# Squares of layer 1's heads summed by two fp32r steps in place of one fp32 matmul

## The reference, cut to what matters

```
proj = h @ w_in[layer]                       # 2048 -> 8 x 1024
q_sb, k_sb, v_sb, z_sb, q_r, k_r, v_r, z_r = jnp.split(proj, split_at, axis=-1)
qa = rms_norm(split_heads(q_sb, 8), sb_q_gain)      # mean of squares over the 128 of a head
ka = rms_norm(split_heads(k_sb, 8), sb_k_gain)
oa = merge_heads(stick_breaking_attention(qa, ka, v)) * silu(z_sb)
...
ob = head_group_norm(chunkwise_retention(qr, kr, vr), ret_norm_gain)   # variance over the 128 of a head
ob = ob * silu(z_r)
x = x + gate * (concatenate([oa, ob]) @ w_out)
```

## Time and profile before

| | us |
|---|---|
| runs | 1768.15, 1771.90, 1775.87 |
| profiled execution, its own time | 1773.34 |
| its span | 1771.5 |
| PE busy | 1726.1 (97%) |
| DVE busy | 1293.4 (73%) |
| ACT busy | 906.5 (51%) |
| POOL busy | 152.3 (9%) |

### The profile page before, as it was taken

The page is one execution under the profiler, slowest core; times in us unless marked ns, Lnnn a source line. Parts: engine busy times, 40 slices in busy tenths (PEclk is TensorE's granted clock), DMA queues, the critical chain, the costliest instruction groups (busy, mean ns, idle before and its releaser), DMA issues.

```text
span 1771.5 us, 24147 instructions
## 1 busy us (share of the span) xinstructions
PE 1726.1 (97%) x9557; PEld 1482.4 (84%) x9557; DVE 1293.4 (73%) x1618; ACT 906.5 (51%) x1176; POOL 152.3 (9%) x177
## 2 busy tenths in 40 slices
PE   7989999999999999999999999999999999999997
PEld 6778888777888888888888888788888888888886
DVE  6889979786788756887677778965554767778653
ACT  6344443444466445665345566644444445566543
POOL 3321101010010100101010010000000000000000
PEclk9989999999999999999999999999999999999999
DMA  9979979774555566667676556556566665544553
GB/s 359 384 273 344 343 228 325 235 242 140 165 167 176 183 178 190 183 186 215 178 215 191 165 167 172 170 185 188 180 186 167 171 197 144 142 131 132 168 188 107
DMA packets 312287, 357.00 MB, mean 202 GB/s; under 512 B 11632, under 2 KB 285168, under 8 KB 312176
## 3 DMA queue, kind: packets, MB, share of 16 engines
q1 hardware_dynamic: 295792, 296.24, 55.3%
q0 software_dynamic: 16384, 59.22, 9.8%
HBM read 353.29 MB, written 2.13 MB: 201 GB/s over the span
## 4 chain that ended last, share of the span: by engine, by line
PE 73%; DVE 14%; ACT 6%; issue 3%; DMA 2%; POOL 1%; SPq 0%; DVEq 0%; ACTq 0%
PE psG L491 41%; PE psG L492 21%; DVE w_lo L421 5%; ACT w_hi L417 3%; PE psG L485 2%; PE psG L487 2%; PE psG L486 2%; DMA raw<-in_mem_w 2%; DVE ada_sum L1289 1%; PE psH L1899 1%; DVE P L1247 1%; PE psH L1913 1%; DVE P L1242 1%; PE psH L1888 0%; PE psH L2079 0%
## 5 line engine op out<-in xcount | busy, mean ns | idle before, releaser
L491 PE MATMUL psG<-xA,w_hi 128*128 128x512 f32 x2624 | 944.4, 403 | 2.5 <-DVE w_lo L421 1.9
L421 DVE TENSOR_TENSOR w_lo<-raw,w_hi 128x1024 fp32r<-128x1024 f32 (+1 forms) x560 | 686.2, 1238 | 228.5 <-ACT w_hi L417 227.0
L492 PE MATMUL psG<-xA,w_lo 128*128 128x256 f32 x2624 | 736.4, 281 | 0.0
L417 ACT ACTIVATE w_hi<-raw 128x1024 fp32r<-128x1024 f32 (+1 forms) x560 | 569.4, 1042 | 238.5 <-PE psG L492 176.4
L491 PEld LDWEIGHTS psG<-xA,w_hi 128*128 128x128 f32 x2624 | 494.4, 188 | 122.2 <-issue 6.3
L492 PEld LDWEIGHTS psG<-xA,w_lo 128*128 128x128 f32 x2624 | 496.9, 189 | 2.3 <-issue 1.4
L491 PE MATMUL psG<-yP,w_hi 128*128 128x512 f32 x960 | 340.6, 399 | 3.4 <-DVE P L1247 1.6
L492 PE MATMUL psG<-yP,w_lo 128*128 128x256 f32 x960 | 269.4, 281 | 0.0
L491 PEld LDWEIGHTS psG<-yP,w_hi 128*128 128x128 f32 x960 | 180.2, 188 | 48.0 <-DVE P L1247 1.9
L460 ACT ACTIVATE P<-psG 128x512 f32<-128x512 f32 (+2 forms) x103 | 60.8, 591 | 239.4 <-PE psG L492 239.4
L492 PEld LDWEIGHTS psG<-yP,w_lo 128*128 128x128 f32 x960 | 181.4, 189 | 0.2
(11 more groups left out here) (331 smaller groups left out, 1777.0 us busy)
## 6 DMA issues: line engine op xcount, KB each, us to landing
raw<-in_w_in SPq DMA_DIRECT2D x360, 512.0 KB, 3.8
raw<-in_w_out SPq DMA_DIRECT2D x128, 512.0 KB, 3.5
ada_ring<-in_w_ada POOLq DMA_DIRECT2D x96, 512.0 KB, 6.2
raw<-in_mem_w SPq DMA_DIRECT2D x32, 512.0 KB, 10.3
raw<-in_w_uq SPq DMA_DIRECT2D x24, 384.0 KB, 3.5
raw<-in_w_ukv SPq DMA_DIRECT2D x32, 128.0 KB, 2.5
raw<-in_w_ukv SPq DMA_DIRECT2D x16, 256.0 KB, 3.4
P<-in_memT SPq DMA_DIRECT2D x4, 512.0 KB, 7.2
```

What stands on the lines that cost most here:

```text
L417: nc.scalar.activation(high(n), low(n, raw), ACT.Copy).then_inc(hi_ready, 1)
L421: nc.vector.tensor_tensor(low(n), low(n, raw), high(n), ALU.subtract).then_inc(lo_ready, 1)
L491: nc.tensor.matmul(psG[:, bank + f, :], hi[:, w], x, start=first, stop=False)
L492: last = nc.tensor.matmul(psG[:, bank + f, S:2 * S], lo[:, w], x[:, 0:S], start=False, stop=end)
```

## The change

The squares are split into a high part in fp32r (ACT, by a copy) and the exact remainder (DVE, by a subtraction), and PE sums both parts with a matrix of ones in fp32r, accumulating into the same bank. `WR` is an fp32r name for the memory of `W`: the high part lies in the second half, the remainder replaces the squares in the first. PE's step moves from p = 2 to p = 3 (retention: p = 12 to 13), ACT's Ln and Exp from p = 3 to 4 (13 to 14). The four semaphores of the dt step are merged into one that counts to 4.

```diff
+        WR = sb("WR", [NP, 2048], F32R, place=top[0])
         W = sb("W", [NP, 2048])
+        ones_r = sb("ones_r", [NP, NP], F32R)
...
@@ ACT
             landed(act, G_SBQK)
+            f(ones_r[:, :], ones, ACT.Copy).then_inc(q["sb_sqh"], 1)
...
                     f(sb_a[:, 512:1024], tiles(n * 2 + SBK, 2), ACT.Square).then_inc(q["sb_sq"], 1)
-                if p == 3:
+                    act.wait_ge(q["sb_sq"], 2 * n + 2)
+                    f(WR[:, 1024:2048], sb_a, ACT.Copy).then_inc(q["sb_sqh"], 1)
+                if p == 4:
                     act.wait_ge(q["sb_ssq"], n + 1)
...
                     f(rt_a[:, 512:1024], rt_a[:, 0:512], ACT.Square).then_inc(q["rt_sq"], 1)
-                if p == 13:
+                    act.wait_ge(q["rt_sq"], n + 1)
+                    f(WR[:, 1024:1536], rt_a[:, 512:1024], ACT.Copy).then_inc(q["rt_sqh"], 1)
+                if p == 14:
                     act.wait_ge(q["rt_var"], n + 1)
@@ DVE
+                if p == 1:
+                    dve.wait_ge(q["sb_sqh"], n + 2)
+                    v.tensor_tensor(WR[:, 0:1024], sb_a, WR[:, 1024:2048], ALU.subtract).then_inc(q["sb_sql"], 1)
...
+                if p == 13:
+                    dve.wait_ge(q["rt_sqh"], n + 1)
+                    v.tensor_tensor(WR[:, 512:1024], rt_a[:, 512:1024], WR[:, 1024:1536], ALU.subtract).then_inc(q["rt_sql"], 1)
@@ PE
-                if p == 2:
-                    pe.wait_ge(q["sb_sq"], n * 2 + 2)
+                if p == 3:
+                    pe.wait_ge(q["sb_sql"], n + 1)
                     if n:
                         pe.wait_ge(q["sb_y"], n)
-                    mm(psH[:, BB, :], ones, sb_a[:, 0:512], start=True, stop=True)
-                    mm(psH[:, BC, :], ones, sb_a[:, 512:1024], start=True, stop=True).then_inc(q["sb_ssq"], 1)
+                    for k in range(2):
+                        mm(psH[:, BB + k, :], ones_r[:, :], WR[:, 1024 + 512 * k:1536 + 512 * k], start=True, stop=False)
+                        ins = mm(psH[:, BB + k, :], ones_r[:, :], WR[:, 512 * k:512 * k + 512], start=False, stop=True)
+                    ins.then_inc(q["sb_ssq"], 1)
...
-                if p == 12:
-                    pe.wait_ge(q["rt_sq"], n + 1)
-                    mm(psH[:, BD, :], ones, rt_a[:, 512:1024], start=True, stop=True).then_inc(q["rt_var"], 1)
+                if p == 13:
+                    pe.wait_ge(q["rt_sql"], n + 1)
+                    mm(psH[:, BD, :], ones_r[:, :], WR[:, 1024:1536], start=True, stop=False)
+                    mm(psH[:, BD, :], ones_r[:, :], WR[:, 512:1024], start=False, stop=True).then_inc(q["rt_var"], 1)
```

More of the change, by code:

```diff
@@ L235, in build @@
             "gate_log gate_lsig gate_sig silc_e ada_cols gate_cols nm_sq nm_pair nm_pre nm_ss nm_ln nm_rs nm_h nm_hi nm_lo "
-            "sb_sq sb_ssq sb_ln sb_rs sb_qk sb_z sb_zs sb_az sb_e sb_l sb_sp sb_S sb_arg sb_w sb_o sb_y "
-            "rt_t0 rt_s rt_qk rt_D rt_z rt_at rt_o rt_os rt_vc rt_sq rt_var rt_ln rt_rs rt_y "
-            "f1_yz f1_y f1_hi f1_lo dt_abs dt_ln dt_cum dt_T mem_col "
+            "sb_sq sb_sqh sb_sql sb_ssq sb_ln sb_rs sb_qk sb_z sb_zs sb_az sb_e sb_l sb_sp sb_S sb_arg sb_w sb_o sb_y "
+            "rt_t0 rt_s rt_qk rt_D rt_z rt_at rt_o rt_os rt_vc rt_sq rt_sqh rt_sql rt_var rt_ln rt_rs rt_y "
+            "f1_yz f1_y f1_hi f1_lo dt_step mem_col "
             "cv_acc cv_tap cv_a cv_e cv_l cv_b cv_s cv_done xt xd_done "
@@ L631, in _ @@
                   .then_inc(q["cv_done"], 1)
-            pool.wait_ge(q["dt_T"], 1)
+            pool.wait_ge(q["dt_step"], 4)
             pool.dma_start(sums_out[:, :], P[0:SSD_HEADS, CUM, :]).then_inc(sums_stored, 16)
@@ L913, in dt_hook @@
                 if bb == 0 and p == 3:
-                    act.wait_ge(q["dt_abs"], 1)
+                    act.wait_ge(q["dt_step"], 1)
                     link(f(P[0:32, DTP + 1, :], P[0:32, DTP + 1, :], ACT.Exp, scale=-1.0))
                     link(f(col[0:32, 2:3], vec[0:32, VEC["a_log"]:VEC["a_log"] + 1], ACT.Exp))
-                    f(P[0:32, DTP + 1, :], P[0:32, DTP + 1, :], ACT.Ln, bias=1.0).then_inc(q["dt_ln"], 1)
+                    f(P[0:32, DTP + 1, :], P[0:32, DTP + 1, :], ACT.Ln, bias=1.0).then_inc(q["dt_step"], 1)
             def conv_hook(v, p):
@@ L1516, in dt_hook @@
                     landed(dve, G_DT)
-                    v.scalar_tensor_tensor(out=e, in0=t, scalar=-1.0, in1=t, op0=ALU.mult, op1=ALU.max).then_inc(q["dt_abs"], 1)
+                    v.scalar_tensor_tensor(out=e, in0=t, scalar=-1.0, in1=t, op0=ALU.mult, op1=ALU.max).then_inc(q["dt_step"], 1)
                 if bb == 0 and p == 6:
-                    dve.wait_ge(q["dt_ln"], 1)
+                    dve.wait_ge(q["dt_step"], 2)
                     link(v.scalar_tensor_tensor(out=t, in0=t, scalar=0.0, in1=e, op0=ALU.max, op1=ALU.add))
@@ L1526, in dt_hook @@
                     v.tensor_scalar(e[:, 0:NP], cum[:, 0:NP], cum[:, NP - 1:NP], -1.0, ALU.subtract, ALU.mult)\
-                     .then_inc(q["dt_cum"], 1)
+                     .then_inc(q["dt_step"], 1)
                 if bb == 0 and p == 11:
-                    dve.wait_ge(q["dt_T"], 1)
+                    dve.wait_ge(q["dt_step"], 4)
                     v.tensor_copy(P[:, SCOL, 0:160], psH[:, BA, 0:160])
@@ L2040, in dt_hook @@
                 if bb == 0 and p == 10:
-                    pe.wait_ge(q["dt_cum"], 1)
+                    pe.wait_ge(q["dt_step"], 3)
                     cum, dt = P[0:32, CUM, :], P[0:32, DTP, :]
@@ L2044, in dt_hook @@
                         ins = turn(psH[:, BA, 32 * k:32 * k + 32], x, 32)
-                    ins.then_inc(q["dt_T"], 1)
+                    ins.then_inc(q["dt_step"], 1)
             run_products(pe, G_SZ0, dt_hook)
```

## The result

The changed kernel takes 1781.3 us in the median of 19 runs (1772.41 to 1786.07), the kernel before 1771.9 us (19 runs). The ratio is 1.0056, 95% interval 1.0043 to 1.0068: slower by 9.9 us (7.6 to 12.0), forecast 9.2. Of the 35 runs of the kernel before that stand beside experiments 5 to 8, one took 4513 us and is left out of their ratios. The interval holds the forecast and also rival 3 (+7.9); it leaves out rivals 1 and 2 (-4.7, +1.5) and, narrowly, rival 4 (+12.6).

A forecast was written before the change was run, and what follows sets the result against it. PE is 97% busy, but in `sb_hook` the chain through ACT and DVE arrives last. Terms: `sb_hook` 6.4, retention 1.5, clock 1.3, together 9.2 us on 1771.9, giving 1781.1 us (+0.52%); range 1773 to 1786.

The forecast's parts named there:

- rival 3: The forecast's chain of delays without the clock's fall: +7.9 us, 1779.8 us; chance 0.30.
- Rival 1: All of PE's matmul saving is kept: -4.7 us, 1767.2 us; chance 0.04.
- rival 2: Waits at p = 3 come, but Ln's delay is absorbed before p = 12: +1.5 us, 1773.4 us; chance 0.13.
- rival 4: Clock falls also behind waits of about 2.0 us at p = 12, n = 1 and 2: +12.6, 1784.5; chance 0.20.
- PE's saving: fp32r sums save 0.78 us in each `sb_hook` iteration, 0.39 in each `rt_hook` iteration: 4.7 us in all.
- The path of 4.44 us behind L829: `sb_hook`, from the end of L829: copy, hi(3), lo(3), subtraction in series take 4.44 us before PE's sum.
- the steps named: PE waits at the new sum (p = 3) 0 / 0.9 / 1.1 / 3.0 us in n = 0 to 3; more at p = 12.
- Ln's delay comes out at p = 12 in full: `sb_hook`: Ln's lateness reaches p = 12 undiminished (n = 3: counted at p = 7); four iterations add 6.4 us.
- The sizes: `sb_hook` delays by iteration: n = 0 +0.63, n = 1 +1.53, n = 2 +1.69, n = 3 +2.6 us.
- Retention: `rt_hook`: PE waits 1.13 us at its sum in n = 2; lateness reaches the last heads' gating, +1.5 us.
- The clock: PE's clock falls once behind the 3.0 us wait in `sb_hook` n = 3: +1.3 us at p = 7.

The follow-up runs named there:

- e4: Kernel before with `sb_hook` squares written as fp32r and summed twice by fp32r matmuls at p = 2, no split, outputs not the reference's: 1767.55 us, ratio 0.9990.
- e5: The change with DVE's subtraction of `sb_hook` at p = 0, ahead of lo(3), instead of p = 1: 1775.69 us, ratio 1.0031 to the kernel before.
- e3: Kernel before with its fp32 sums, only PE's `sb_hook` sum moved from p = 2 to 3 and ACT's Ln from 3 to 4: 1774.94 us, ratio 1.0034.
- e2: The change in `rt_hook` (retention) alone, `sb_hook` as in the kernel before: 1771.06 us, ratio 1.0002 to the kernel before.
- e1: The change in `sb_hook` alone, retention as in the kernel before: 1781.49 us, ratio 1.0068 to the kernel before.
- e6: The whole change with DVE's L1385 moved from p = 11 to p = 10, ahead of lo(8): 1775.65 us, ratio 1.0026 to the kernel before.
- e7: Kernel before with only DVE's L1385 moved from p = 11 to p = 10, ahead of lo(8): 1766.19 us, ratio 0.9978 to the kernel before.
- e8: The change in `sb_hook` with the subtraction at p = 0 and L1385 at p = 10, retention as before: 1768.20 us, ratio 0.9991 to the kernel before.

## Why the prediction was right

- **PE's saving**: 0.78 us for each pair of sums, right. e4 shows -3.1 for the stage, and the matmuls start 0.23 apart.
- **The path of 4.44 us behind L829**: 4.44 in n = 1. The waits came at the steps named. e5 takes two links out of the path and the waits of n = 1 and 2 go.
- **Ln's delay comes out at p = 12 in full**: shown by e3, where nothing but the places of the sum and of Ln was changed, and against rival 2, which needed slack there. From p = 15 of n = 0 to that of n = 3 I forecast +5.8, +7.1 with the clock; it is +7.30. The waits at p = 12 of n = 1 and 2 are 1.72 and 1.83, forecast about 2.
- **The sizes**: n = 1 and 2 were sized 0.12 and 0.16 too low, because Ln comes 1.23 us after the start of a sum that had waited (350.32 to 351.55), where I had 1.12: the first matmul behind a wait is followed after 0.33, not 0.23.
- **Retention**: +1.5 forecast, +1.75 in the change's profile and +1.7 in e2's. Its wait in n = 2 was 0.95 for 1.13. The runs of e2 can't show it, and no experiment moved a step of this part: its path is read from the rows alone.
- **The clock**: I gave rival 3, the chain without it, nearly the forecast's chance. All three profiles with the wait of 3.0 us in n = 3 (the change, e1, e6) have the low stretch behind it; none of the seven others (before, e2, e3, e4, e5, e7, e8) has one there, nor does any behind the waits of 1.7 to 1.8 at p = 12, so rival 4 falls too. It isn't only the profiles: over all their 39 runs the three kernels have a mean granted clock of 0.9891, the others over their 137 runs 0.9905, and 0.0014 of 1771 us is an estimated 2.5 us, where the stretch costs 1.7. What it costs at p = 7 can be read at either level: from the sum to p = 7 of n = 3 are 8.12, 8.08 and 8.11 us in the three, 6.95 in e5 and 6.96 in e8, whose clock stayed at 1.00. That is 1.2 us, forecast 1.3, and leaves 2.7 of the 3.90 for the path, forecast 2.6.
- **Luck**: 9.6 from the distances and 9.9 from the runs lie closer than the runs' interval (7.6 to 12.0) warrants, and the halves show it: e1 and e2 gave 12.0 and 0.4 where the distances say 7.9 and 1.7. The runs alone don't tell the forecast from rival 3.
- **Rival 1**, all of the saving kept, was the reading of the busy shares alone. e4 is what it would take, e2 and e3 what speaks against it.

Not separated: how much of the loss in n = 3 is due to ACT's wait for the last gate addition, which starts that path late. By the rows, the second square ends 5.49 us after p = 15 of n = 2, against 3.39 and 3.44 us after the p = 15 ahead of n = 1 and 2; so an estimated 2.1 of the 3.0 us at the sum are due to it. No run took that wait away.

## What to carry to other kernels

An engine at 97% can still be waiting for a chain through engines at 50 to 75%, and then an edit is priced by what it does to the chain's next handoff: list all that stands in the queues between the new producer and its consumer. Here 1.06 us of copy and 1.22 us of subtraction became 4.4 us of path, because two unrelated splits stood between them. Before work is added to save PE's time, try the free edit: moving one existing instruction past a split it need not wait for brought more in that stage (3.7 us by the distances) than PE's whole saving there (3.1).

## What the runs showed of the hardware that was not expected

- The idle time shown for PE understates a wait. Taking away waits that read 0.65, 0.78 and 0.95 us shortened p = 7 to p = 12 by 0.95, 0.94 and 1.11 us (e7), and in n = 3, where no wait was shown, by 0.19.
- Executions agree to about 0.1 us in distances between starts within a stage (p = 7 to 12 of n = 1: 9.19 before, 9.20 in e2, which does not touch it), while whole executions of one kernel spread over 13 us (1762.91 to 1776.30). Part of that is the clock: of the runs of the kernel before that stand beside the experiments, the five with a mean granted clock of 0.987 or less took 1774.3 us on the mean, the eleven with 0.993 or more 1767.2.
- The clock behind the gate's one-column matmuls falls in some executions and not in others. The low stretch is in the profile of before at 315 and at 438 us, in the change's at neither; of the ten profiles six have one at the first place and five at the second. From p = 15 of the last `sb_hook` iteration to the scores of the first retention iteration are 15.42 to 15.53 us with it and 13.85 to 14.04 without: about 1.5 us.
